# One table set with both logarithm and exponential in front of each ScalarE chain of the two

## The reference

```
def _rmsnorm(x, g, eps=NORM_EPS):
    xf = x.astype(jnp.float32)
    y = xf * lax.rsqrt(jnp.mean(xf * xf, axis=-1, keepdims=True) + eps)
    return (y * g.astype(jnp.float32)).astype(x.dtype)
...
    kk = kk / jnp.maximum(jnp.linalg.norm(kk, axis=-1, keepdims=True), 1e-12)
...
    y = ((y - mean) * lax.rsqrt(var + RWKV_GN_EPS)).reshape(B, S, RWKV_DIM) * ln_w + ln_b
```

## Time and profile before

| what | value |
|---|---|
| median of three runs | 3587.93 us (3586.98 to 3589.36) |
| the profiled execution's own time | 3588.55 us |
| span of its trace | 3586.8 us |
| TensorE matmul busy | 3375.5 us, 94% |
| VectorE busy | 1796.2 us, 50% |
| ScalarE busy | 1324.2 us, 37% |
| mean granted TensorE clock | 0.973 of full speed |

### The profile page before, as it was taken

The page is one execution under the profiler, slowest core; times in us unless marked ns, Lnnn a source line. Parts: engine busy times, 40 slices in busy tenths (PEclk is TensorE's granted clock), DMA queues, the critical chain, the costliest instruction groups (busy, mean ns, idle before and its releaser), DMA issues.

```text
span 3586.8 us, 45528 instructions
## 1 busy us (share of the span) xinstructions
PE 3375.5 (94%) x19392; PEld 2680.2 (75%) x19392; DVE 1796.2 (50%) x2920; ACT 1324.2 (37%) x2125; POOL 105.4 (3%) x202
## 2 busy tenths in 40 slices
PE   6898978999999899999899999999999989999998
PEld 4767755887888688887567788878887756778887
DVE  4545665566757465644654533343333465443333
ACT  4341465534525432223443322233223344332222
POOL 0000000010000010100000000000000000000000
PEclk9999989999999999999999999999999989999999
DMA  3010111454443265633112222222222211222221
GB/s 134 26 43 20 45 40 55 155 193 168 147 158 141 88 235 200 233 124 113 51 48 77 83 100 94 100 77 101 99 94 102 105 50 48 71 83 97 97 96 69
DMA packets 100538, 363.99 MB, mean 101 GB/s; under 512 B 11632, under 2 KB 11696, under 8 KB 99696
## 3 DMA queue, kind: packets, MB, share of 16 engines
q1 hardware_dynamic: 75888, 272.14, 21.0%
q0 software_dynamic: 24448, 88.95, 7.1%
HBM read 358.94 MB, written 2.10 MB: 101 GB/s over the span
## 4 chain that ended last, share of the span: by engine, by line
PE 87%; DVE 8%; ACT 4%; issue 1%; DMA 0%; DVEq 0%; ACTq 0%; POOL 0%; POOLq 0%
PE ps_run L414 85%; PE ps_run L695 1%; DVE nrm L1730 1%; ACT L1060 1%; ACT nrm L1060 1%; DVE HL L1730 1%; DVE wl L1723 1%; ACT wh L1060 0%; DVE ug L1723 0%; DVE AL L1723 0%; DVE nst L2341 0%; ACT ug L1060 0%; DMA vec<-vec 0%; ACT nP L1060 0%; DVE cp L1723 0%
## 5 line engine op out<-in xcount | busy, mean ns | idle before, releaser
L414 PE MATMUL ps_run<-HH,wh 128*128 128x512 f32 x2608 | 1052.7, 404 | 61.3 <-DVE HL L1730 35.9
L414 PE MATMUL ps_run<-HL,wh 128*128 128x512 f32 x2608 | 1026.9, 394 | 0.0
L414 PE MATMUL ps_run<-HH,wl 128*128 128x512 f32 x2608 | 1026.6, 394 | 0.0
L1723 DVE TENSOR_TENSOR wl<-st,wh 128x1024 fp32r<-128x1024 f32 x511 | 625.1, 1224 | 762.8 <-ACT wh L1060 762.6
L1060 ACT ACTIVATE wh<-st 128x1024 fp32r<-128x1024 f32 x511 | 537.9, 1054 | 715.8 <-PE ps_run L414 710.8
L414 PEld LDWEIGHTS ps_run<-HH,wh 128*128 128x128 f32 x2608 | 496.2, 190 | 193.6 <-DVE HL L1730 58.1
L414 PEld LDWEIGHTS ps_run<-HL,wh 128*128 128x128 f32 x2608 | 497.6, 191 | 104.6 <-issue 7.0
L414 PEld LDWEIGHTS ps_run<-HH,wl 128*128 128x128 f32 x2608 | 496.5, 190 | 105.8
L414 PE MATMUL ps_run<-AH,wh 128*128 128x512 f32 x1104 | 431.0, 390 | 0.0
L414 PE MATMUL ps_run<-AH,wl 128*128 128x512 f32 x1104 | 429.7, 389 | 0.0
L414 PE MATMUL ps_run<-AL,wh 128*128 128x512 f32 x1104 | 429.5, 389 | 0.0
(11 more groups left out here) (405 smaller groups left out, 3302.9 us busy)
## 6 DMA issues: line engine op xcount, KB each, us to landing
st<-wst SPq DMA_DIRECT2D x511, 512.0 KB, 3.2
mb<-ada POOLq DMA_DIRECT2D x144, 512.0 KB, 4.4
cw<-cw POOLq DMA_DIRECT2D x4, 1024.0 KB, 6.2
X<-xT SPq DMA_DIRECT2D x8, 256.0 KB, 9.4
X<-xT POOLq DMA_DIRECT2D x8, 256.0 KB, 5.1
out<-X SPq DMA_DIRECT2D x8, 256.0 KB, 2.1
kc<-kc POOLq DMA_DIRECT2D x1, 1139.0 KB, 7.3
mb<-cond POOLq DMA_DIRECT2D x2, 512.0 KB, 5.1
```

Of the source, the lines that this page charges most:

```text
L414: i = self.e.matmul(out, lhsT, rhs, start=start, stop=stop, skip_group_check=True)
L1723: self.e.tensor_tensor(out, a, b, op).then_inc(*self.w.done(*points))
```

## The change

`table` no longer evaluates a function: it puts a load of the set that holds both the logarithm and the exponential there. Two calls are added, one in `rwkv_front` (once per half-front, for stream 0) ahead of the exponentials, one in `diff` behind the sine and cosine.

```
     def table(self):
-        self.act(self.m.junk, self.m.C("ones", 0, 1), ACT.Ln)
+
+        self.e.preload_act_table_set("natural_log_exp_and_others")
...
         self.act(s["sq"], s["kk"], ACT.Square, (q, "kk squared"))
         yield
+        if st == 0:
+            self.table()
         w.wait_ge(q, "cp")
         self.act(s["c"], s["L"], ACT.Exp)
...
             self.act(out, out, ACT.Sin, (name,))
+        self.table()
 
         def exps(n):
```

## The result

The changed kernel took 3562.47 us, median of 4 runs (3562.11 to 3564.75), against 3588.47 us for the kernel before (4 runs, 3586.98 to 3589.36): ratio 0.9929, 95% interval 0.9914 to 0.9945. A second comparison later gave 0.9941 (0.9923 to 0.9958). The runs of the kernel before scatter from 3582.5 to 3592.6 us, those of the changed one from 3562.1 to 3572.2, so that a difference of a few us has to be read in the traces.

What follows compares the result with a forecast made beforehand. The chain that ended last was 87% TensorE, so ScalarE's loads count only on it. Terms 11.0 + 0.7 + 1.3 + 4.4 + 0 + 2.2 = 19.6 us gave 3568.4 us; forecast 3564 to 3572.5, 8-in-10 range 3562 to 3576.

Steps and rivals of the forecast that it cites:

- the clock adds to it: Rival: shorter TensorE gaps let some differential-attention groups run at the upper clock, 3 to 5 us on top; chance 0.10.
- A load on the path is worth 1.22 us: Between a norm's logarithm and exponential on ScalarE: 1.31 us less 0.09 for ScalarE's own wait; nine such places, 11.0 us.
- First end 1.3 us: Recurrence's first end: ScalarE gains 2.6 us, but VectorE then waits for raw, leaving 1.3 us; bounds 1.2 and 2.6.
- Half-fronts zero: Recurrence's half-fronts: eight removed loads, none on the chain, hidden under TensorE's projections of 20.01 and 20.95 us; gain zero.
- Second end 4.4 us: Recurrence's second end: four loads in series; ScalarE gains 4.8 us, TensorE only its gaps, 4.4 us; bounds 3.1 and 4.8.
- the sign of being wrong that I had named: Profile after: the prediction would be wrong if the second end's gap on TensorE stays (one of three signs).
- The moved load cancels: Differential attention's start: squares delayed 1.4 us, offset by the load gone before the first mr logarithm; zero, bounds -1.3 and +1.3.
- Second small norm 2.2 us: Differential attention's second mr: both loads go, dP could start 2.6 us earlier; 2.2 us taken, between 1.8 and 2.6.
- TensorE's busy time hardly changes: Expected in the profile after, over the whole kernel: TensorE's busy time stays nearly the same.
- only the plain places pay: Rival: waits replace the loads in recurrence and differential attention, leaving 11.7 us, so 3576.2 us; chance 0.13.
- drain: Rival: a load holds ScalarE longer than its record, 23 us more would come back, 3545 us; chance 0.01.
- slow set: Rival: the combined set is fetched from memory, seven preloads x 3.2 = 22.4 us, 3590.8 us; chance 0.02 for slower.

Runs made afterwards that it cites:

- the two calls alone: Changed kernel with the helper evaluating into junk as before, only the two added calls loading the combined set (58 loads): 3580.99 us, ratio 0.9984.

## Why the prediction was right, and its size low

The main mechanism, that a load counts where ScalarE is on the path and then counts its record, was right; in the stages of short turns two terms came out near their size for reasons that were partly others. The time, 3562.5 us, lies below the forecast's own 3564 to 3572.5 and within what the rival *the clock adds to it* (0.10) had named, down to 3559; the wider range held it because it took in part of that rival. Point by point:

- *A load on the path is worth 1.22 us*: it is worth 1.28, the own wait costing 0.03 and not 0.09. Over nine norms and the loads of the ends that would be 0.8 us more. Seven of the nine norms' stages gained 1.25 to 1.30 us on the mean of three traces; but all nine together gained 10.8 where 11.2 were forecast, since the first norm gained 1.0 and the stage of the first layer's mixer 0.9.
- *Added loads hidden*: right; the one before `ld` has 2.0 us to spare, and the one before the tangent on `wa` 0.24.
- *First end 1.3 us*: 1.2, and `raw` takes the rest of the 2.6 us, as forecast. That the whole recurrence up to the second scan gained 1.2 us too is luck. *Half-fronts zero* holds only as a sum: one stretch gained 1.2 us and another lost as much, with TensorE's busy time.
- *Second end 4.4 us*: 4.9 by VectorE's marks, 5.3 with what follows. ScalarE's own gain, 4.8, was the upper bound, and VectorE got it in full. But the 4.4 was the sum of TensorE's gaps, and these did not vanish, 2.4 us of masks are left: the sign of being wrong that I had named stands in part. At the second mask's matmul, 384.99 us before and 377.67 after, TensorE's lead over the trace of before had grown by 3.4 us, from 3.97 to 7.32, mostly from gaps. It grew by another 1.6 within the next 4 us, in matmuls alone, of which some had run at the lower level before and now ran at the upper one. So the size came out near 4.4 in part by luck.
- *The moved load cancels*: not in full. The step up to the first small norm took 12.9 us in the three traces before and 14.3, 13.1 and 13.2 after, 0.2 to 1.4 us more. Putting the load back behind the squares gained 0 to 1.1 us on the stage.
- *Second small norm 2.2 us*: the rest of the stage took 26.9, 25.9 and 26.9 us before and 23.2, 23.3 and 23.7 after, 3.2 us less on the mean, above the bound of 2.6. The stage as a whole has 2.5, near 2.2 because the two misses offset each other.
- *TensorE's busy time hardly changes*: wrong. It fell from 3375.5 to 3367.5 us with the same matmuls, by 6.9 us on the mean of three traces against three. I had put the clock into a rival at 0.10 and into the differential attention's start. That stage has 1.6 us of it, with a granted clock of 0.64, 0.72 and 0.64 before and 0.69, 0.77 and 0.73 after, and the second end with the projections behind it 2.4. The largest part, 3.2, came where nothing was changed, in the second layer's mixer; in all, that stage is 3.5 us shorter on the mean of three traces, 5.3 in the pair first profiled.
- The rival *only the plain places pay* falls with the second end and with the two calls alone; the *drain* falls with the norms, which lost a load that switched the set and gained its record and no more; the *slow set* with the 17 loads of 1283 ns.

So the stages that it named gave 20.7 us against 19.6, and that small difference hides the misses above, which partly offset. The step that was mis-sized is TensorE's busy time, which the sum left at nothing: it has a share in the 20.7, and it makes the 2.3 us of the two unchanged stages, where it fell by 2.7; what is left to the measured 26.0 is the scatter of the start and of the runs. That the changed kernel has the mixer at 192.5 us in two of three traces and the kernel before at 197.9 in two of three is shown; the 197.9 stands in no trace of any other kernel. That it moved to 191.06 in both traces with a load ahead of it is shown; why the mixer starts where the clock treats it so, I can't say. A part of the gain therefore hangs on this kernel's other times and may go with the next edit.

## What to carry to other kernels

Look up each table load in the chain of work that ended last, and count its record, here 1.28 us, for each one that stands in it; the others were free here, added ones too, where the engine would have been idle anyway. Where two functions alternate on the path, load one set with both ahead of the chain, and then look for the loads that are left there (here four more in series, worth 6 us with the evaluation between them and the faster matmuls behind).

Where three engines pass work in short turns, compare at least two traces of each kernel stage by stage before giving a stage's difference a cause: a stage with the same instructions differed here by 3 us between two executions of one program, and by 10 us between the traces of two kernels.

## What the runs showed of the hardware

- A table load took 1283 ns in all fourteen traces, whichever set, also for the set that was loaded already. The page "ScalarE: Activation LUTs" of the Trainium skill (section "What ACT_TABLE_LOAD costs") gives this figure; the 1380 ns of drain that it adds for each switch to a different set do not appear on this path: taking the switch away saved 1.28 us per norm.
- Two dependent ScalarE evaluations of 128x512 with a wait of the engine for itself between them stood 0.03 us apart, at all 19 places in each of three traces.
- In both traces with a delay of 1.28 us ahead of the second mixer it was given back in full, with a higher granted clock (0.94 against 0.93) in the 191 us behind it.
- In latent attention a stretch with the same 138 matmuls took 19.5 us at a granted clock of 1.00 in twelve traces, 21.1 at 0.92 in one and 27.7 at 0.63 in another.
- The 16 matmuls for a norm's sums took 9.49 us behind 7.21 us in which TensorE did nothing, at a granted clock of 0.79, and 7.69 behind 3.06, at 1.00.
